# State space mixer: the order of a chunk's work on all engines, forward values in two buffers a chunk ahead, the norm's root on columns

## The chip, the cores and the metric

The kernel runs on one NeuronCore of a Trainium2 chip. The metric is the device time of one launch in microseconds (us), and lower is better. Five engines work side by side: PE (TensorE, the matmuls, with PEld as its weight loads), DVE (VectorE), ACT (ScalarE), POOL (GpSimd) and SP (SyncE, which issues DMAs). Each runs its own instructions strictly in order; semaphores tie them together.

## What is computed

Two transformer-like blocks over 512 tokens and 256 context tokens of width 1024, all in float32. The change touches one of the mixers only, the state space mixer of the first block. Per head h (32 heads of 64 channels, in 4 groups g of 8 heads), per direction d (forward and backward), and per chunk c of 128 tokens:

```python
acs = cumsum(dt * a)                                            # per chunk
chunk_state = einsum('cgs,cge,cgep->geps', bm, exp(a_last - acs), x * dt)
state = exp(a_last) * state + chunk_state                       # chunk by chunk
decay = exp(where(tril, acs_i - acs_j, -inf))
y_diag = einsum('gij,geij,jgep->igep', cm @ bm.T, decay, x * dt)
y_off  = einsum('cgs,geps,cge->cgep', cm, s_start, exp(acs))
...
y = (yf + flip(yb) + d_skip * xs) * silu(z)
yg = y.reshape(tokens, 4, 512)                                  # a group's 512 channels
y = yg * rsqrt(mean(yg * yg, -1) + 1e-6) * norm_w
out = y @ w_out
```

The 256 context tokens give two chunks that only feed the state; the other four chunks give outputs.

## The kernel before

The class `Ssd` makes the mixer. `steps` writes the order down by hand, as one list of steps; every engine walks the whole list and does its own part of each step (`tensor`, `vector`, `scalar`, `pool`, `sync`). So where a step stands in the list sets where it stands on all engines at once. PSUM has eight banks; `banks.take` gives a step a bank, with a wait for whoever read that bank last. The weight panels (`Weights`) are brought by SP, rounded by ACT (`RWH<-RW`, 1.05 us) and their rest is taken by DVE or POOL (`RWr<-RW,RWH`, 1.2 and 2.4 us); where those stand is set by a look-ahead in steps, which the table `calm` shortens in places.

A group g goes through three parts.

- **Convolution.** `cin`, `tap`, `silu`, `ctr`: six column blocks of the input product, taps on DVE, transposes. The steps `third` are the first of the next group's `cin`, cut in three pieces that are put in as filler of PE.
- **States.** For x = 0 to 4, `st` (DVE scales the values into `w1`; PE multiplies, one for each direction) and `sa` (DVE adds to the state). Between them stand the pieces `z` of the gate's product, 12 matmuls of 128x512 each.
- **Chunks**, c = 0 to 3. `ct` and `cb`: small matmuls, whose results ACT copies to `BD`, `NJ` (five small ACTIVATEs) and `cbr`, and POOL masks into `cb`. `gp`: four matmuls with 8 rows into four banks G. `gm`: ACT copies two of the banks to `GG[c % 2]`, DVE takes the minimum with the other two, ACT takes the exponential. `gc`: DVE multiplies that by `cb`, once for each direction, into `GF` (one buffer) and in place (two TENSOR_TENSOR of 128x1024). `xd`: the values times dt, POOL the forward ones, DVE the backward ones. `yd`: 16 matmuls, eight for a direction, with values and masked products. `yo` and `off`: the state's share, on PE, scaled by DVE and added up on POOL in `yy`; `skip` on POOL starts that sum. `ot`: four matmuls that add `yy` to the bank of `yd`. `ya`: DVE multiplies by the gate, ACT squares.

Then the norm, for two halves j of 256 tokens: `ss` on PE sums the squares (four matmuls of 128x256 with the matrix `mean`, which gives every row the sum), ACT takes the root of 128x256 values, DVE their reciprocal (`self.rq`), and `yf` multiplies (DVE), rounds (ACT) and splits (POOL) for the output product `mix`.

The forward values have one buffer (`self.xd[0]`), so POOL's product for chunk c waits until `yd` of chunk c - 1 has read it:

```python
            if c:
                gp.wait_ge("pe.ssd", "yd", g, c - 1)
            else:
                gp.wait_ge("pe.ssd", "S", g, 0, 4)
            gp.wait_ge("v.ssd_dt", "dt")
            gp.tt(self.heads(self.xd[0]), self.heads(self.xs[:, c, :]), self.each(self.DT[:, c, 8 * g:8 * g + 8]),
                  ALU.mult).then_inc("g.ssd_xd", g, c)
            for n in (0, 1) if c == 0 else (c + 1,) if c < 3 else ():
                self.skip(gp, g, n)
```

In the trace nearly everything is recorded in helpers: line 107 is a matmul, 118 and 121 ACTIVATEs, 124 a TENSOR_TENSOR, 138 a reciprocal. The tiles tell the steps apart: `G<-G` and `A<-G,TM` belong to `gm` and `gc`, `PS<-A,TM 128*64` to `yd`. In the group-by-group rows, a matmul in float32 has two records.

Of the kernel before, what the change touches and what calls it, by code (L numbers as in the profile page):

```python
# [1823 lines left out]
class Ssd(Stage):  # L1824
# [6 lines left out]
    def __init__(self, k, gen):  # L1831
# [26 lines left out]
        self.rq = (a(10752, 256), a(11008, 256))  # L1858
# [5 lines left out]
        self.KK = k.dst[:, 0:10]  # L1864
        self.units = [(c, d) for c in range(4) for d in range(2)]

    def steps(self, mixes, mod):
# [4 lines left out]
        last = []  # L1872
        for g in range(4):
# [76 lines left out]
    def tensor(self, p, step, *a):  # L1950
# [94 lines left out]
        elif step == "yd":  # L2045
            g, c = a
            pv = k.banks.take(p, 1, "ssd", "yd", g, c)
            for d, gg in enumerate((self.GF, self.GG[c % 2])):
                p.wait_ge("v.ssd_G", g, c, d)
                p.wait_ge(("g.ssd_xd", "v.ssd_xd")[d], g, c)  # L2050
                for h in range(8):
                    m, half = h // 2, slice(64 * (h % 2), 64 * (h % 2) + 64)
                    last = p.mm(pv[half, 128 * m:128 * m + 128], self.xd[d][:, 64 * h:64 * h + 64], gg[:, h, :],
# [9 lines left out]
        elif step == "ss":  # L2063
# [3 lines left out]
            for m in range(4):  # L2067
                last = p.mm(pv[:, 0:256], k.mean[:, :], self.zz[:, m, 256 * j:256 * j + 256], m == 0, m == 3)
            last.then_inc("pe.ssd", "ss", g, j)

    def scalar(self, s, step, *a):
# [81 lines left out]
        elif step == "gm":  # L2153
# [18 lines left out]
        elif step == "ss":  # L2172
            g, j = a
            if g:
                s.wait_ge("v.ssd_yf", g - 1, j)
# [1803 lines left out]
```

## Time and profile before

| | us |
|---|---|
| median of 3 runs | 4063.89 (4057.85 to 4063.95) |
| the profiled execution | 4055.57 |
| its span | 4053.8 |
| PE busy in it | 3824.3 (94%) |
| DVE, ACT, POOL busy | 1621.4, 1408.8, 1147.2 |

The mixer takes the time from about 1216 to 1875 us of the span. PE carries the chain of waits that ended last (79% of it), so what counts is time in which PE waits or runs at the lower of its two clock levels (2.4 and 1.2 GHz; a granted clock of 1.00 and 0.50). Busy times of PE overlap a little from one matmul to the next, so lengths below are taken from one start to the next.

### The profile page before, as it was taken

The page shows a single profiled execution, that of the slowest core. Times are in us where ns is not written, and L with a number is a line of the kernel's source. Part 1 is how long each engine was busy: PE and PEld are TensorE (multiplying, and loading weights), DVE is VectorE, ACT ScalarE, POOL GpSimd, SP SyncE. Part 2 cuts the span into 40 slices and gives each one's busy share as a digit, 9 for nine tenths or more (in the row PEclk, how much of TensorE's full clock was granted, in tenths as well). Part 3 has the DMA queues.
Part 4 walks back from the last instruction along what each step waited for, and adds up shares of the span by engine and source line. Part 5 has one row for each costly group of instructions (what it writes and reads, how often), then busy time and mean ns, then how long its engine had stood idle before and what let it go on. Part 6 is the DMA issues. An engine that isn't in the chain of part 4 may idle for free.

```text
span 4053.8 us, 52334 instructions
## 1 busy us (share of the span) xinstructions
PE 3824.3 (94%) x22125; PEld 3161.7 (78%) x22125; DVE 1621.4 (40%) x2600; ACT 1408.8 (35%) x2209; POOL 1147.2 (28%) x689
## 2 busy tenths in 40 slices
PE   7999889999999899897999999999998889999999
PEld 5777667888887677676888788888877766688887
DVE  4355573111136666666212321111457843332123
ACT  4223344211125433434422332211455536443223
POOL 2010013111123423425222421211434413243324
PEclk9999999999999999999999999999999999999999
DMA  5221123332333121123333412222322210152333
GB/s 181 73 80 32 58 92 122 97 96 92 96 104 87 33 67 47 33 63 130 107 105 101 151 53 67 64 63 60 117 72 67 59 44 29 55 151 73 99 95 108
DMA packets 472117, 336.66 MB, mean 83 GB/s; under 512 B 17754, under 2 KB 445772, under 8 KB 471884
## 3 DMA queue, kind: packets, MB, share of 16 engines
q1 hardware_dynamic: 471200, 333.06, 27.0%
q8 instruction: 175, 2.87, 0.3%
q14 instruction: 59, 0.48, 0.0%
q10 hardware_dynamic: 683, 0.26, 0.0%
HBM read 331.17 MB, written 2.10 MB: 82 GB/s over the span
## 4 chain that ended last, share of the span: by engine, by line
PE 79%; DVE 8%; ACT 5%; POOL 3%; DMA 2%; issue 2%; SPq 0%; ACTq 0%; POOLq 0%; DVEq 0%
PE PS L107 77%; DVE A L124 2%; PE PS L115 1%; POOL TM L124 1%; ACT A L118 1%; ACT L118 1%; DVE A L132 1%; POOL RWr L124 1%; DMA MW<-in_w_ada 1%; ACT RWH L121 1%; DMA MW<-in_mod_w 1%; DVE TM L132 1%; DVE XT L124 1%; DVE SM L144 1%; ACT TM L118 0%
## 5 line engine op out<-in xcount | busy, mean ns | idle before, releaser
L124 POOL TENSOR_TENSOR RWr<-RW,RWH 128x1024 fp32r<-128x1024 f32 (+2 forms) x316 | 728.4, 2307 | 2235.8 <-ACT RWH L121 2233.1
L107 PE MATMUL PS<-HTH,RWH 128*128 128x512 f32 (+1 forms) x3488 | 1262.7, 362 | 20.8 <-POOL RWr L124 7.6
L107 PE MATMUL PS<-HTH,RWr 128*128 128x512 f32 (+1 forms) x3488 | 1228.1, 352 | 0.0
L107 PE MATMUL PS<-HTr,RWH 128*128 128x512 f32 (+1 forms) x3488 | 1227.9, 352 | 0.0
L107 PE MATMUL PS<-Ar,RWH 128*128 128x512 f32 (+1 forms) x3264 | 819.6, 342 | 20.2 <-DVE XT L132 7.1
L107 PEld LDWEIGHTS PS<-HTH,RWH 128*128 128x128 f32 x3488 | 665.9, 191 | 144.2 <-issue 43.9
L107 PEld LDWEIGHTS PS<-HTr,RWH 128*128 128x128 f32 x3488 | 666.4, 191 | 89.5 <-issue 6.5
L107 PEld LDWEIGHTS PS<-HTH,RWr 128*128 128x128 f32 x3488 | 664.9, 191 | 90.6 <-issue 0.4
L107 PEld LDWEIGHTS PS<-Ar,RWH 128*128 128x128 f32 x3264 | 563.8, 191 | 108.4 <-issue 18.1
L121 ACT ACTIVATE RWH<-RW 128x1024 fp32r<-128x1024 f32 (+2 forms) x474 | 474.8, 1006 | 310.7 <-DMA RW<-in_ffn_w_out 164.9
L107 PE MATMUL PS<-Ar,RWr 128*128 128x512 f32 (+1 forms) x1632 | 552.8, 339 | 0.0
L124 DVE TENSOR_TENSOR A<-A,PS 128x512 f32<-128x512 f32 (+2 forms) x192 | 138.2, 725 | 812.9 <-PE PS L107 801.5
L124 DVE TENSOR_TENSOR RWr<-RW,RWH 128x1024 fp32r<-128x1024 f32 (+2 forms) x158 | 201.5, 1275 | 594.0 <-ACT RWH L121 593.9
L107 PE MATMUL PS<-A 128*128 128x128 f32 (+5 forms) x1820 | 316.8, 360 | 52.8 <-DVE A L124 19.4
L107 PEld LDWEIGHTS PS<-Ar,RWr 128*128 128x128 f32 x1632 | 311.3, 191 | 33.6
L107 PEld LDWEIGHTS PS<-A 128*128 128x128 f32 (+2 forms) x1820 | 216.3, 193 | 137.2 <-issue 66.7
L121 ACT ACTIVATE Ar<-A 128x512 fp32r<-128x512 f32 (+3 forms) x124 | 89.6, 723 | 562.4 <-DVE A L124 529.8
L118 ACT ACTIVATE A<-PS 128x512 f32<-128x512 f32 (+1 forms) x132 | 90.4, 688 | 504.5 <-PE PS L107 492.7
L132 DVE SCALAR_TENSOR_TENSOR XT<-PS,M,XT 128x512 f32<-128x512 f32 (+1 forms) x200 | 117.8, 618 | 275.6 <-PE PS L107 275.3
L121 ACT ACTIVATE A<-PS 128x256 f32<-128x256 f32 (+4 forms) x224 | 115.7, 542 | 278.4 <-PE PS L107 206.2
L118 ACT ACTIVATE A<-A 128x512 f32<-128x512 f32 (+3 forms) x152 | 101.3, 681 | 262.2 <-DVE A L124 175.1
L118 ACT ACT_TABLE_LOAD x129 | 165.5, 1283 | 31.8 <-PE PS L107 18.9
(189 smaller groups left out, 3403.5 us busy)
## 6 DMA issues: line engine op xcount, KB each, us to landing
RW<-in_ffn_w_in SPq DMA_DIRECT2D x176, 512.0 KB, 3.8
MW<-in_mod_w SPq DMA_DIRECT2D x83, 512.0 KB, 4.6
MW<-in_w_ada SPq DMA_DIRECT2D x72, 512.0 KB, 4.5
RW<-in_ffn_w_out SPq DMA_DIRECT2D x64, 512.0 KB, 3.6
RW<-in_ffn_w_out SPq DMA_DIRECT2D x64, 384.0 KB, 3.2
RW<-in_mix_w_in SPq DMA_DIRECT2D x41, 512.0 KB, 3.7
RW<-in_ssd_w_in SPq DMA_DIRECT2D x40, 512.0 KB, 3.9
RW<-in_ev_w_in SPq DMA_DIRECT2D x24, 512.0 KB, 3.8
```

Source lines behind the costliest of these rows:

```text
L107: return self._ins(self.real and self.real.matmul(o, l, r, start=start, stop=stop, skip_group_check=True))
L115: return self._ins(self.real and self.real.transpose(o, i, self.k.ident[0:n, 0:n]))
L118: return self._ins(self.real and self.real.activation(o, i, f, **kw))
L121: return self._ins(self.real and self.real.activation(o, i, ACT.Copy))
L124: return self._ins(self.real and self.real.tensor_tensor(out=o, in0=i0, in1=i1, op=op))
L132: return self._ins(self.real and self.real.scalar_tensor_tensor(out=o, in0=i0, scalar=sc, in1=i1, op0=op0, op1=op1))
L144: return self._ins(self.real and self.real.reduce_max(o, i, AX.X))
```

## The change

Four things change in `Ssd`, and one number in `plan`.

1. `steps`: `gp` of chunk 0 moves out of x = 4 to behind x = 3, with `ct` and `cb` of chunk 1; all eight pieces of `z` now stand in the state steps. `gp` of chunk c + 2 stands at the end of turn c (before, `gp` of chunk c + 1 stood at the start of it). `yo` of chunk c + 1 stands ahead of `yd` of chunk c. The last turn does `ot` and `ya` ahead of the second filler.
2. The step `gx` is new: it holds the two copies by ACT that stood in `gm`, and directly follows `gp`.
3. The forward values get two buffers, `xdf`, and the new function `value` makes chunk c + 1's in the step `xd` of chunk c.
4. The norm's sums become columns: `ss` has eight matmuls that leave 128x1 each, root and reciprocal are taken on 128x2 values, and a new step `sp` spreads them again with two matmuls of 128x128; `yf` reads that bank.
5. `calm`'s entry for the state steps is 12 in place of 24, and covers `gp` of chunk 0.

```diff
-        self.rq = (a(10752, 256), a(11008, 256))
+        self.root = (k.dst[:, 12:14], k.dst[:, 14:16])
+        self.xdf = (work[:, 0:512], a(10752, 512))
...
             for x in range(5):
-                out += one("st", g, 0, x) + one("st", g, 1, x)
-                out += one("gp", g, 0) + one("yo", g, 0) if x == 4 else z[x + 3]
-                out += one("sa", g, 0, x) + one("sa", g, 1, x)
-            out += one("gm", g, 0) + z[7] + one("yo", g, 1) + one("xd", g, 0) + one("off", g, 0) + one("off", g, 1)
-            out += one("ct", g, 1) + one("cb", g, 1) + one("yo", g, 2) + one("yo", g, 3)
+                out += one("st", g, 0, x) + one("st", g, 1, x) + z[x + 3] + one("sa", g, 0, x) + one("sa", g, 1, x)
+                if x == 3:
+                    out += one("gp", g, 0) + one("gx", g, 0) + one("ct", g, 1) + one("cb", g, 1)
+            out += one("gm", g, 0) + one("yo", g, 0) + one("yo", g, 1) + one("gp", g, 1) + one("gx", g, 1) + one("xd", g, 0)
...
-                turn = one("gp", g, c + 1) if more else self.filler(g, 0, mod)
-                turn += one("gc", g, c) + one("yd", g, c)
+                turn = [] if more else self.filler(g, 0, mod)
+                if c == 0:
+                    turn += one("off", g, 0) + one("off", g, 1)
+                turn += one("gc", g, c)
                 if more:
-                    turn += one("off", g, 2 * c + 2) + one("gm", g, c + 1) + one("off", g, 2 * c + 3)
-                else:
-                    turn += self.filler(g, 1, mod)
+                    turn += one("yo", g, 2 * c + 2) + one("yo", g, 2 * c + 3) + one("gm", g, c + 1)
+                turn += one("yd", g, c)
+                if more:
+                    turn += one("off", g, 2 * c + 2) + one("off", g, 2 * c + 3)
                 if c < 2:
                     turn += one("ct", g, c + 2) + one("cb", g, c + 2)
-                turn += one("ot", g, c) + one("ya", g, c)
                 if more:
                     turn += one("xd", g, c + 1)
+                turn += one("ot", g, c) + one("ya", g, c)
                 if c < 2:
-                    turn += one("yo", g, 2 * c + 4) + one("yo", g, 2 * c + 5)
+                    turn += one("gp", g, c + 2) + one("gx", g, c + 2)
                 if c == 2:
                     turn += one("ss", g, 0)
                 if c == 3:
-                    turn += one("yf", g, 0)
+                    turn += self.filler(g, 1, mod) + one("sp", g, 0) + one("yf", g, 0)
                 turns.append(turn)
-            turns += [one("ss", g, 1), one("yf", g, 1)]
+            turns += [one("ss", g, 1), one("sp", g, 1) + one("yf", g, 1)]
...
-            for m in range(4):
-                last = p.mm(pv[:, 0:256], k.mean[:, :], self.zz[:, m, 256 * j:256 * j + 256], m == 0, m == 3)
+            for c in range(2):
+                for m in range(4):
+                    at = 256 * j + 128 * c
+                    last = p.mm(pv[:, c:c + 1], self.zz[:, m, at:at + 128], k.ones[:, 0:1], m == 0, m == 3)
...
+            p.wait_ge("v.ssd_rs", g, j)
+            for c in range(2):
+                last = p.mm(pv[:, 128 * c:128 * c + 128], self.root[j][:, c:c + 1].to_broadcast([128, 128]), k.ident,
+                            True, True)
...
+    def value(self, gp, g, c):
...
+        if c > 1:
+            gp.wait_ge("pe.ssd", "yd", g, c - 2)
+        else:
+            gp.wait_ge("pe.ssd", "S", g, 1, 4)
+        gp.tt(self.heads(self.xdf[c % 2]), self.heads(self.xs[:, c, :]), self.each(self.DT[:, c, 8 * g:8 * g + 8]),
+              ALU.mult).then_inc("g.ssd_xd", g, c)
...
-            k.w.calm.update((i, 24) for i, step in enumerate(steps) if step[0] is ssd and (
-                step[1] == "z" and step[3] or step[1] in ("st", "sa") and step[4]))
+            k.w.calm.update((i, 12) for i, step in enumerate(steps) if step[0] is ssd and (
+                step[1] == "z" and step[3] or step[1] in ("st", "sa") and step[4] or step[1] == "gp" and not step[3]))
```

DVE in the last two turns of group 0, before, from `gc` of chunk 2 on: `A<-A,PS` or `G<-G,PS` is `gm`, `TM<-PS,TM` and `A<-PS,TM` are `off` of the two directions, `A<-PS,A` is `ya`, `TM<-A,TM` is `xd`, `A<-A,TM 128x1024` is `gc`.

```order
747 L124 TENSOR_TENSOR A<-G,TM 128x1024
748 L124 TENSOR_TENSOR G<-G,TM 128x1024
749 L124 TENSOR_TENSOR TM<-PS,TM 128x512
750 L124 TENSOR_TENSOR A<-A,PS 128x512 x2
751 L124 TENSOR_TENSOR A<-PS,TM 128x512
752 L124 TENSOR_TENSOR A<-PS,A 128x4x128
753 L124 TENSOR_TENSOR TM<-A,TM 128x512
754 L138 RECIPROCAL A<-A 128x256
755 L124 TENSOR_TENSOR RWr<-RW,RWH 128x1024
756 L124 TENSOR_TENSOR A<-A,TM 128x1024 x2
757 L124 TENSOR_TENSOR A<-PS,A 128x4x128
758 L132 SCALAR_TENSOR_TENSOR A<-A,VEC 128x256 x4
```

The same place on DVE after:

```order
747 L124 TENSOR_TENSOR A<-G,TM 128x1024
748 L124 TENSOR_TENSOR G<-G,TM 128x1024
749 L124 TENSOR_TENSOR A<-A,PS 128x512 x2
750 L124 TENSOR_TENSOR TM<-PS,TM 128x512
751 L124 TENSOR_TENSOR A<-PS,TM 128x512
752 L124 TENSOR_TENSOR TM<-A,TM 128x512
753 L124 TENSOR_TENSOR A<-PS,A 128x4x128
754 L124 TENSOR_TENSOR RWr<-RW,RWH 128x1024
755 L124 TENSOR_TENSOR A<-A,TM 128x1024 x2
756 L124 TENSOR_TENSOR A<-PS,A 128x4x128
757 L138 RECIPROCAL SM<-SM 128x2
758 L132 SCALAR_TENSOR_TENSOR A<-A,VEC,PS 128x256 x4
```

The minimum now stands ahead of both `off`, `xd` ahead of `ya`, and the reciprocal, now 128x2, behind the last `gc` and `ya`.

POOL in the chunks of group 1, before: `TM<-A,CC` masks `cb`, the first of `TM<-A,TM` is the forward value, the next the skip; `TM<-TM`, `TM<-TM,A`, and `A<-A,TM`, `A<-A` are `off`'s sums (an `A<-A,TM` ahead of them is a skip too).

```order
78 L124 TENSOR_TENSOR TM<-A,TM 128x512 x2
79 L124 TENSOR_TENSOR A<-A,TM 128x512
80 L124 TENSOR_TENSOR TM<-TM 128x512
81 L124 TENSOR_TENSOR TM<-TM,A 128x512
82 L124 TENSOR_TENSOR TM<-A,CC 128x256
83 L124 TENSOR_TENSOR A<-A,TM 128x512
84 L124 TENSOR_TENSOR A<-A 128x512
85 L124 TENSOR_TENSOR TM<-A,CC 128x256
86 L124 TENSOR_TENSOR TM<-A,TM 128x512 x2
87 L124 TENSOR_TENSOR TM<-TM 128x512
```

POOL, the same place after:

```order
77 L124 TENSOR_TENSOR TM<-A,TM 128x512 x2
78 L124 TENSOR_TENSOR A<-A,TM 128x512
79 L124 TENSOR_TENSOR TM<-TM 128x512
80 L124 TENSOR_TENSOR TM<-TM,A 128x512
81 L124 TENSOR_TENSOR A<-A,TM 128x512 x2
82 L124 TENSOR_TENSOR A<-A 128x512
83 L124 TENSOR_TENSOR TM<-A,CC 128x256
84 L124 TENSOR_TENSOR TM<-A,TM 128x512 x2
85 L124 TENSOR_TENSOR TM<-TM 128x512
```

The first three rows are now the value and skip of chunk 0 and the value of chunk 1; the skip of chunk 1 has moved behind the first two sums, and only one mask stands between the sums of chunk 1 and the next value, which is chunk 2's (row 84; row 86 of before is chunk 1's).

## Rows read from the trace of the kernel before

**Rows 1.** Windows of the four chunk stretches: from:to, length, busy by engine, granted clock, DMA.

```profile
1354.20:1404.10 49.90, 41.27 (x283) 28.70 (x283) 33.61 (x34) 24.86 (x45) 31.07 (x21) 0.86 0.07 22
1511.20:1557.50 46.30, 38.57 (x282) 26.58 (x282) 33.74 (x35) 24.74 (x45) 31.47 (x21) 0.93 0.07 24
1663.20:1710.90 47.70, 38.84 (x282) 26.53 (x282) 34.58 (x35) 24.81 (x45) 31.45 (x21) 0.93 0.07 23
1816.40:1850.70 34.30, 28.96 (x220) 18.15 (x220) 27.81 (x30) 22.28 (x43) 31.01 (x21) 0.95 0.09 32
```

**Rows 2.** Timeline, PE, group 1: start, us, form, count, idle before and releaser.

```profile
1511.18 2.20 PE L107 MATMUL PS<-A 8*128 8x512 f32 x10
1512.81 0.79 PE L107 MATMUL PS<-HTH,RWH 128*128 128x512 f32 x1
...
1515.99 1.02 PE L107 MATMUL PS<-A 128*128 128x512 f32 x2
...
1520.82 1.09 PE L107 MATMUL PS<-A,TM 128*64 128x128 f32 x16
...
1522.71 0.41 PE L107 MATMUL PS<-CC,TM 128*8 128x128 f32 x8
...
1530.24 3.40 PE L107 MATMUL PS<-A,TM 128*64 128x128 f32 x32 [2.71 <-POOL TM L124]
...
1539.32 1.33 PE L107 MATMUL PS<-A,TM 128*64 128x128 f32 x16 [1.25 <-ACT A L121]
...
1543.83 1.89 PE L107 MATMUL PS<-A,mean 128*128 128x256 f32 x8
...
1551.72 1.53 PE L107 MATMUL PS<-A,TM 128*64 128x128 f32 x20 [3.27 <-DVE A L124]
```

**Rows 3.** Timeline, POOL, group 1: value of chunk 1 and skip of chunk 2.

```profile
1528.07 3.02 POOL L124 TENSOR_TENSOR TM<-A,TM 128x512 f32<-128x512 f32 x2
```

**Rows 4.** Timeline, DVE, group 1: `gm`, `xd`, `gc` of chunk 1, reciprocal, `gc` of chunk 3.

```profile
1521.89 1.27 DVE L124 TENSOR_TENSOR A<-A,PS 128x512 f32<-128x512 f32 x2
...
1525.08 1.32 DVE L124 TENSOR_TENSOR TM<-A,TM 128x512 f32<-128x512 f32 x1
1526.32 2.88 DVE L124 TENSOR_TENSOR A<-A,TM 128x1024 f32<-128x1024 f32 x2
...
1547.21 1.75 DVE L138 RECIPROCAL A<-A 128x256 f32<-128x256 f32 x1 [1.66 <-ACT A L118]
1548.88 3.87 DVE L124 TENSOR_TENSOR A<-A,TM 128x1024 f32<-128x1024 f32 x2
```

**Rows 5.** Timeline, PE, group 0: `yd` of chunk 1.

```profile
1374.48 3.68 PE L107 MATMUL PS<-A,TM 128*64 128x128 f32 x32 [3.27 <-POOL TM L124]
```

**Rows 6.** Timeline, ACT, group 1: table load and exponentials, then `ct`'s five.

```profile
1513.49 1.28 ACT L118 ACT_TABLE_LOAD   x1
1514.79 1.16 ACT L118 ACTIVATE G<-G 128x512 f32<-128x512 f32 x2
...
1524.40 1.84 ACT L118 ACTIVATE A<-PS,SM 128x128 f32<-128x128 f32 x5
```

**Rows 7.** Timeline, two layer norms: sums, modulation row, root, reciprocal, spread.

```profile
1223.64 1.84 PE L107 MATMUL PS<-ones,TM 128*128 128x1 f32 x16
1225.41 0.64 PE L107 MATMUL PS<-MW,CS 128*32 128x256 f32 x8
...
1904.99 0.26 ACT L118 ACTIVATE SM<-PS,cols 128x2 f32<-128x2 f32 x1 [1.37 <-PE PS L107]
1905.28 0.17 DVE L138 RECIPROCAL SM<-SM 128x2 f32<-128x2 f32 x1 [0.66 <-ACT SM L118]
...
1907.58 0.71 PE L107 MATMUL PS<-CC,SM 128*128 128x128 f32 x4
```

**Rows 8.** Timeline, PE, group 3 behind its chunks: a modulation row.

```profile
1864.72 0.64 PE L107 MATMUL PS<-MW,CS 128*32 128x256 f32 x8 [1.85 <-DMA MW<-in_w_ada]
```

**Rows 9.** Windows of PE around two waits of 1.25 us: busy, clock.

```profile
1540.00:1543.40 3.40, 3.40 (x29) 0.51 0.02 5
...
1844.00:1847.20 3.20, 1.95 (x30) 1.00 0.00 0
```

More of the change, by code:

```diff
@@ L2050, in tensor @@
                 p.wait_ge(("g.ssd_xd", "v.ssd_xd")[d], g, c)
+                xd = self.xd[1] if d else self.xdf[c % 2]
                 for h in range(8):
                     m, half = h // 2, slice(64 * (h % 2), 64 * (h % 2) + 64)
-                    last = p.mm(pv[half, 128 * m:128 * m + 128], self.xd[d][:, 64 * h:64 * h + 64], gg[:, h, :],
+                    last = p.mm(pv[half, 128 * m:128 * m + 128], xd[:, 64 * h:64 * h + 64], gg[:, h, :],
                                 not d and h < 2, False)
@@ L2066, in tensor @@
             p.wait_ge("s.ssd_sq", g, 2 * j + 1)
-            for m in range(4):
-                last = p.mm(pv[:, 0:256], k.mean[:, :], self.zz[:, m, 256 * j:256 * j + 256], m == 0, m == 3)
+            for c in range(2):
+                for m in range(4):
+                    at = 256 * j + 128 * c
+                    last = p.mm(pv[:, c:c + 1], self.zz[:, m, at:at + 128], k.ones[:, 0:1], m == 0, m == 3)
             last.then_inc("pe.ssd", "ss", g, j)
+        elif step == "sp":
+            g, j = a
+            pv = k.banks.take(p, 1, "ssd", "sp", g, j)
+            p.wait_ge("v.ssd_rs", g, j)
+            for c in range(2):
+                last = p.mm(pv[:, 128 * c:128 * c + 128], self.root[j][:, c:c + 1].to_broadcast([128, 128]), k.ident,
+                            True, True)
+            last.then_inc("pe.ssd", "sp", g, j)
     def scalar(self, s, step, *a):
@@ L2163, in scalar @@
                     "s.ssd_gb", g, c, x).frees("ssd", "G", g, c, 2 + x)
+        elif step == "gm":
+            g, c = a
+            gg = self.GG[c % 2]
             for x in range(2):
@@ L2173, in scalar @@
             g, j = a
-            if g:
-                s.wait_ge("v.ssd_yf", g - 1, j)
             s.wait_ge("pe.ssd", "ss", g, j)
-            s.act(self.rq[j], k.banks.of("ssd", "ss", g, j)[:, 0:256], ACT.Sqrt, bias=k.epsc, scale=2.0).then_inc(
+            s.act(self.root[j], k.banks.of("ssd", "ss", g, j)[:, 0:2], ACT.Sqrt, bias=k.epsc, scale=1.0 / 512).then_inc(
                 "s.ssd_rs", g, j).frees("ssd", "ss", g, j)
@@ L2267, in vector @@
             if i % 2 == 0:
-                if g and i == 0:
-                    v.wait_ge("v.ssd_yf", g - 1, 1)
                 v.wait_ge("pe.ssd", "ctr", g, i)
@@ L2347, in vector @@
                  self.zz[:, :, cs], ALU.mult).then_inc("v.ssd_y", g, c).frees("ssd", "yd", g, c)
-        elif step == "ss":
+        elif step == "sp":
             g, j = a
             v.wait_ge("s.ssd_rs", g, j)
-            v.rcp(self.rq[j], self.rq[j]).then_inc("v.ssd_rs", g, j)
+            v.rcp(self.root[j], self.root[j]).then_inc("v.ssd_rs", g, j)
         elif step == "yf":
@@ L2377, in pool @@
             g, c = a
-            self.xs_ready(gp, g)
-            if c:
-                gp.wait_ge("pe.ssd", "yd", g, c - 1)
-            else:
-                gp.wait_ge("pe.ssd", "S", g, 0, 4)
-            gp.wait_ge("v.ssd_dt", "dt")
-            gp.tt(self.heads(self.xd[0]), self.heads(self.xs[:, c, :]), self.each(self.DT[:, c, 8 * g:8 * g + 8]),
-                  ALU.mult).then_inc("g.ssd_xd", g, c)
             for n in (0, 1) if c == 0 else (c + 1,) if c < 3 else ():
-                self.skip(gp, g, n)
+                self.value(gp, g, n)
+                if n != 1:
+                    self.skip(gp, g, n)
         elif step == "off":
@@ L2394, in pool @@
             gp.tt(yy, yy, self.yo[d], ALU.add).then_inc("g.ssd_off", g, i)
+            if i == 1:
+                self.skip(gp, g, 1)
         elif step == "yf":
```

10 lines of the change are left out of this document (6 added, 4 removed).

## Prediction

> **What bounds the kernel now.** Start with the table: PE is busy 94% of the span, and the chain of waits runs through it. So the question is how long PE waits in the stretches that the change touches, and at which clock it runs there. I read four views in this order. The windows [rows 1] cut out the chunk stretch of each group, from the start of `gp` of chunk 0 to the start of the third `third` piece (in group 3 to the first modulation matmuls): 49.9, 46.3, 47.7 and 34.3 us, at granted clocks of 0.86, 0.93, 0.93 and 0.95. PE is busy 8.6, 7.7, 8.9 and 5.3 us less than that. The timeline of PE [rows 2, 5] names the waits of a group: 2.71 us (3.27 in group 0) ahead of `yd` of chunk 1, released by POOL (the forward value), 1.25 ahead of `yd` of chunk 2, released by ACT (the exponential), 3.27 ahead of `yd` of chunk 3, released by DVE (`gc`). The other engines' timelines say why. POOL starts value 1 at 1528.07 [rows 3], since it had to wait for `yd` of chunk 0, and needs half of 3.02. DVE starts the last `gc` only after a reciprocal of 1.75 which itself waited 1.66 for the root [rows 4]. The clock: a mean clock of 0.86 means 28% of the time at half speed, and work done at half speed loses half of its time, 14% of the whole. So 49.9 x 0.14 = 7.0, 46.3 x 0.07 = 3.2, 47.7 x 0.07 = 3.3 and 34.3 x 0.05 = 1.7 us are lost at most, 15.3 in all, in some 30.6 us at the lower level (1.2 GHz).
>
> **Change 1 to 3: the chunks.** Count from t = 0, the end of the last state matmul. `gp` 0, `ct` 1 and `cb` 1 now stand ahead of it; they are 1.14 (a `gp` is 8 records), 0.35 and 0.35, so a stretch has 1.85 to its credit that is only moved. PE then does z7, which takes 3.2 (1512.81 to 1515.99, [rows 2]), `yo` 0 and 1 (1.02 by two records, 0.95 each by starts): 5.1, `gp` 1: 6.2, `yo` 2 and 3: 8.1. On ACT the gate's SiLU follows z7 (0.6, half of a pair's 1.16), then a table load of 1.28 and the exponential of chunk 0, 1.16 [rows 6]: 6.45. Before, that exponential ran beside z7. Now it is the first link, and what is late behind it is `gc`. A `gc` pair took 2.88 and 3.87 beside POOL [rows 4]; I take 3.7 for chunk 0, where POOL has two values, a mask and skips to do: 10.15. `yd` 0 starts with its forward half and waits for the second: it ends at 11.1, after a wait of about 1.1.
>
> Then each turn repeats. DVE: `gm` 1.2 (1.27 as a pair [rows 4]), two `off` 1.2, `xd` 1.0 (0.65 to 1.32), `ya` 0.6, `gc` 3.8: 7.8. PE in the same turn: `ct` 0.35, wait for ACT's five small ACTIVATEs (1.84 [rows 6], with 0.35 of latency on both sides), `gp` 1.1, two `yo` 1.9, `yd` 1.9, `cb` and `ot` inside the ACT time: about 7.4. The first is longer, so DVE carries the turn. Before, the two `yo` stood between `ct` and `gp` and hid the five ACTIVATEs; now about 1.3 us of PE's waiting stands ahead of `gp` of chunk c + 2. The forward value drops out: POOL makes it a chunk ahead, at a time when it waits for nothing on DVE or PE but `yd` of two chunks earlier. It is queued behind fewer steps than before, and two skips wait behind it, for which only `off`'s sums, half a turn later, wait. Two turns end at 25.75. Behind the third `gc` come `gm`, `off`, `xd` and `ya` of the next chunk (4.0) and ACT's square (0.65, half of 1.23 or less): `ss` 0 starts at 30.5, after a wait of some 2.3, since `ya` 2 now stands behind `xd` 3. From there on PE has `ss` 1.77, filler 2.77 (12 matmuls by 0.23), `yd` 3 1.85, `ot` 0.95, filler 2.77, with no wait: the reciprocal is no longer ahead of `gc`, which needs 3.87 from 30 on and has 4.5. End: 40.6, with the credit 42.45. Group 3 ends its stretch behind `ss`: 1.85 + 30.5 + 1.77 = 34.1.
>
> At full clock throughout, that is 49.9 - 42.45 = 7.45, then 3.85, 5.25 and 0.2: **16.7 us** less.
>
> A rule of the Trainium skill speaks on these links. A `gc` pair took 2.88 in one place and 3.87 in another, beside POOL in both [rows 4]. The Trainium skill (SBUF — State Buffer, SBUF: two separate sides) says that DVE and GpSimd take a shared port pair as an exclusive lock, for a whole instruction; two rows of different length agree with that, and by it a `gc` that starts beside two POOL products could take up to two of POOL's, each 1.0 to 1.5, more; rival D would then be the likeliest.
> The other rule is on the table: the exponential starts 0.02 us behind the end of the 1.28 of the load [rows 6]. The Trainium skill (ScalarE: Activation LUTs, What ACT_TABLE_LOAD costs) has a drain of some 1.38 us beside the load, 2.66 in all. The trace disagrees, and leaves this no chance; by the page, `ss` 0 would stand 1.4 later in each group, and 5.5 of the gain would be gone.
>
> **Change 4: the norm.** `ss` has 16 records of one column in place of 8 of 256. Sixteen such took 1.77 (1223.64 to 1225.41 [rows 7]) where the old form took 1.54 (1.89 less the overlap of 0.35 at the next start): +0.23 for each half, already in the stretch for half 0. The spreads: four records took 0.71, 0.54 by starts [rows 7]: 2 x 0.54. `sp` 0 stands behind filler and waits for nothing. `sp` 1 follows `ss` 1 at once, and PE waits for its own end, the root 0.26, two handovers and the reciprocal 0.17 [rows 7]: about 0.65 (between 0.3, if only the two operations count, and 2.3, the 1.37 and 0.66 of idle time in these rows added to them, a path with more in it). Before, the next group's `cin` followed `ss` 1 and hid the long root and reciprocal. Sum for a group: 1.08 + 0.23 + 0.65 = 1.96, three times **5.9**. In group 3 PE waits for DMA ahead of modulation rows (1.85, [rows 8]) and the addition lies under that: 0. Two table loads per group go; none was waited for.
>
> **Change 5: `calm`.** A look-ahead of 12 moves some roundings and rests; no DMA is added. No PE wait for a weight stood in the stretches. One `RWH` (1.05, in the words on the weight panels) ahead of an exponential would cost as much, once per group; one that goes away gains as much. I take 0, and +4 to -4 for the range.
>
> **The clock.** The waits of a group shrink from about 7.6 to 6.3 by my walk (1.1, 1.3, 1.3, 2.3), and the long ones of 2.7 to 3.3 are gone. What the clock does with that isn't shown by one row: after a wait of 1.25 that came soon behind a longer one it stands at 0.51 for 3.4 us, around an equal one in group 3 at 1.00 [rows 9]. I take one such stretch of 3.4 for a group, behind the 2.3: 1.7 x 4 = **6.8** lost.
>
> **Sum.** 16.7 - 5.9 - 6.8 = 4 us less. The profiled execution took 4055.6 with a span of 4053.8, and is 8.3 below the median of the runs shown and 2.3 below the lowest; the difference is carried over to the median as it is: 4063.9 - 4 = **4060**.
>
> **Rivals.** *Faster (B).* Both uncertain terms fall well: shorter waits leave the clock up (2 lost instead of 6.8), and the turns go at PE's 7.4 as `gc` comes nearer to 2.88 (POOL's work is spread evener): 2 x 0.4 x 4 = 3.2. Gain 16.7 + 3.2 - 5.9 - 2 = 12; with the first `gc` also at 2.9, 3 more. 4049 to 4052. For it: full clock around the single 1.25. Against: four waits a group still.
> *Slower (C).* One mechanism, the clock in the chunks: the chip answers to each of the new waits with 3.4 us at the lower level, since they stand 6 to 8 us apart, as the waits in group 1 did [rows 9]. Each costs 1.7. The sum without clock is 10.8; slower by over 8 us needs 19, that is 11 of them; three for a group, 12, cost 20.4: 4073.5. All 16 give 4080. Against: before, waits of 7.6 in a group led to at most 7 us of loss.
> *It doesn't do what it says (D).* The value's wait goes, but the turn stays as long because `gc` on DVE, with POOL's value and skip beside it, ends no sooner: turns of 9, as now (from 1530.24 to 1539.32 [rows 2]). Two turns of 9 instead of 7.8 cost 2.4 x 4 = 9.6: gain 4 - 9.6, 4069.5.
>
> **How the numbers follow.** A measurement of this kernel tells from no change what is over 0.2%, 8.1 us. My sum (A) has 0.45, with its own range of 4055 to 4069; B 0.36; C 0.11; D 0.08. A reaches into faster a little, D into slower half: faster 0.39, same 0.45, slower 0.16. The range from 4046 to 4073 leaves out the outer third of B and most of C.
>
> **What would show it.** In the profile after: no wait on POOL ahead of `yd` 1; a wait of about 1.1 on DVE inside `yd` 0, of 1.3 on ACT ahead of each `gp` of chunks 2 and 3, of 2.3 on ACT ahead of `ss` 0, none ahead of `yd` 3; `sp` 1 with 0.65 on DVE; stretches of about 42.5 us, and 34 in group 3; 8 table loads fewer. Wrong are the steps whose wait differs by over 0.5. The forecast as a whole fails if the clock of the stretches after rises to 0.98 or more (B) or falls below 0.9 (C), or if the turns aren't near 7.8.

## The result and the profile after

The changed kernel takes 4040.0 us (median of 4 runs, 4038.3 to 4042.2) beside 4063.9 before: the ratio is 0.9949 with a 95% interval of 0.9935 to 0.9963, some 21 us (15 to 26). That is faster, by more than what such a measurement can tell from no change, and it lies below the predicted range, which ended at 4046. The forecast of 4060 said no change.

The profiled execution took 4042.2, with a span of 4040.4; before it was 4055.6. So the two profiles lie 13.4 us apart, and the medians 24. The first question is which steps of the walk failed in the 13.4, the second what became of the rest.

The chunk stretches of the changed kernel, from about the start of z7 (the last piece of the gate's product) to the start of the third filler piece (in group 3 to the end of `ss` 0; the cuts are up to 0.3 us off these starts), with the columns of [rows 1]:

```profile
1358.30:1401.30 43.00, 36.78 (x278) 25.45 (x277) 31.94 (x36) 19.44 (x39) 27.23 (x19) 0.96 0.08 25
1515.00:1553.30 38.30, 35.40 (x280) 24.18 (x279) 31.59 (x35) 19.70 (x39) 29.57 (x20) 1.00 0.09 29
1662.50:1700.80 38.30, 35.40 (x280) 24.19 (x279) 31.57 (x35) 19.69 (x39) 29.55 (x20) 1.00 0.08 28
1810.30:1840.30 30.00, 27.09 (x224) 17.02 (x226) 28.27 (x33) 16.15 (x35) 26.87 (x19) 1.00 0.11 37
```

The clock stands at 1.00 in three of the four, where it was 0.93, 0.93 and 0.95. PE is idle 6.2, 2.9, 2.9 and 2.9 us in them, where it was 8.6, 7.7, 8.9 and 5.3.

PE's timeline in group 1 (start, length, form, count, idle before and releaser), which answers to [rows 2]; the first row is in the state part, the next two are `yd` 0's two halves. The row of 28 records at 1528.75 is `gp` 2, two `yo` and the first half of `yd` 1, and 1532.66 is the second half of `yd` 1. Then come `gp` 3 with two `yo`, the first half of `yd` 2, `ss` 0, the first half of `yd` 3, `sp` 0, `ss` 1 and `sp` 1:

```profile
1505.29 3.13 PE L107 MATMUL PS<-TM,A 128*128 128x512 f32 x4 [1.92 <-DVE TM L124]
...
1522.96 1.09 PE L107 MATMUL PS<-A,TM 128*64 128x128 f32 x16
1525.06 1.09 PE L107 MATMUL PS<-G,TM 128*64 128x128 f32 x16 [1.01 <-DVE G L124]
...
1528.75 4.08 PE L107 MATMUL PS<-A 8*128 8x512 f32 x28 [0.95 <-DVE TM L124]
1532.66 1.07 PE L107 MATMUL PS<-A,TM 128*64 128x128 f32 x16
...
1536.33 3.05 PE L107 MATMUL PS<-A 8*128 8x512 f32 x12 [0.95 <-ACT A L118]
...
1539.32 1.09 PE L107 MATMUL PS<-A,TM 128*64 128x128 f32 x16
...
1542.39 1.84 PE L107 MATMUL PS<-ones,A 128*128 128x1 f32 x16
...
1547.03 1.09 PE L107 MATMUL PS<-A 128*64 128x128 f32 x16
...
1552.70 0.61 PE L107 MATMUL PS<-CC,SM 128*128 128x128 f32 x4
...
1556.02 1.84 PE L107 MATMUL PS<-ones,A 128*128 128x1 f32 x16
...
1558.42 0.71 PE L107 MATMUL PS<-CC,SM 128*128 128x128 f32 x4 [0.55 <-DVE SM L138]
```

The wait for POOL ahead of `yd` 1 is gone, and so is that of 3.27 ahead of `yd` 3. There are three waits of about 1 us in the chunks, one of 0.55 for the reciprocal, and a new one of 1.92 in the state part. For the wait ahead of `gp` 2 the row names DVE, but the DVE product that ends there is `xd` 1 (1527.32 to 1528.70), for which `gp` doesn't wait. In both places it needs ACT's five small ACTIVATEs, which end 0.14 us ahead of it:

```profile
1526.77 1.84 ACT L118 ACTIVATE A<-PS,SM 128x128 f32<-128x128 f32 x5
...
1534.35 1.84 ACT L118 ACTIVATE A<-PS,SM 128x128 f32<-128x128 f32 x5
```

Nothing stands ahead of `ss` 0, where the prediction had put 2.3.

The stretches are not all of the mixer. Outside them the clock still falls, behind `sp` 1 of group 0 (after a wait of 0.55 only), behind the 1.92 in the states of group 1, and at the end of group 3. The last three figures of a row are the granted clock, the DMA share and GB/s:

```profile
1405.50:1413.00 7.50, 6.95 (x28) 0.77 0.20 65
1505.20:1512.00 6.80, 6.63 (x20) 0.75 0.00 0
1853.70:1862.00 8.30, 6.81 (x38) 0.59 0.26 86
```

By the way the prediction counts (length times what the clock falls short of 1), these are 1.7, 1.7 and 3.4 us.

Group 0 alone still waits long ahead of `yd` 3. PE first, then DVE at the same place: the weight's rest stands ahead of `gc`, and has itself waited 3.22 for its rounding on ACT:

```profile
1393.46 1.47 PE L107 MATMUL PS<-A 128*64 128x128 f32 x16 [3.35 <-DVE A L124]
1394.65 1.99 PE L107 MATMUL PS<-A,TM 128*64 128x128 f32 x16
```

```profile
1387.10 0.68 DVE L124 TENSOR_TENSOR A<-PS,A 128x512 f32<-128x512 f32 x1
1391.00 1.23 DVE L124 TENSOR_TENSOR RWr<-RW,RWH 128x1024 fp32r<-128x1024 f32 x1 [3.22 <-ACT RWH L121]
```

To compare whole mixers I take the time from the last transposes ahead of the states of group 0 (1331.57 before, 1331.91 after) to the first sums of the next norm (1888.72 and 1874.82). It holds all four groups, and no row of it depends on where a stretch is cut.

| kernel | median, us | ratio to before (95%) | mixer in its profile | clock of the stretches |
|---|---|---|---|---|
| before | 4062 to 4064 | 1 | 557.2 | 0.86 0.93 0.93 0.95 |
| before, another execution | (4073.2, one run) | | 563.3 | 0.93 0.89 0.87 0.91 |
| changed | 4040.0 | 0.9949 (0.9935 to 0.9963) | 542.9 | 0.96 1.00 1.00 1.00 |
| changed, another execution | (4042.3, one run) | | 544.5 | 1.00 1.00 1.00 1.00 |

### The profile page after: what moved, and what is told of

It is laid out like the page before. It is cut to its first block, busy times and chain, and to the rows that moved or that the text cites. A ratio compares the mean times of both kernels' runs of the same rounds, so it can differ in the third digit from the quotient of the medians.

```text
span 4040.4 us, 52541 instructions
## 1 busy us (share of the span) xinstructions
PE 3823.2 (95%) x22221; PEld 3162.3 (78%) x22221; DVE 1614.3 (40%) x2600; ACT 1396.4 (35%) x2201; POOL 1151.6 (29%) x689
## 4 chain that ended last, share of the span: by engine, by line
PE 79%; DVE 8%; ACT 5%; DMA 3%; issue 2%; POOL 2%; SPq 0%; ACTq 0%; DVEq 0%; POOLq 0%
PE PS L107 77%; DVE A L124 2%; PE PS L115 2%; ACT A L118 1%; DVE A L132 1%; ACT L118 1%; POOL RWr L124 1%; DMA MW<-in_w_ada 1%; DVE TM L124 1%; DMA MW<-in_mod_w 1%; ACT RWH L121 1%; POOL TM L124 1%; DVE TM L132 1%; DVE SM L144 1%; DMA RW<-in_ssd_w_in 0%
## 5 line engine op out<-in xcount | busy, mean ns | idle before, releaser
L107 PE MATMUL PS<-A 128*128 128x128 f32 (+7 forms) x1948 | 322.6, 352 | 57.4 <-DVE A L124 22.6
L107 PEld LDWEIGHTS PS<-A 64*128 64x128 f32 (+3 forms) x1948 | 223.1, 188 | 145.2 <-issue 68.5
```

The source lines that it names most:

```text
L107: return self._ins(self.real and self.real.matmul(o, l, r, start=start, stop=stop, skip_group_check=True))
```

## Experiments

**1. Spare matmuls in the waits of the kernel before.** How much of the time is clock? PE is given useless work in two waits of each group (in group 3 in one), and nothing else is touched.

```diff
             pv = k.banks.take(p, 1, "ssd", "yd", g, c)
+            for _ in range((0, 6, 0, 7 if g < 3 else 0)[c]):
+                p.mm(pv[:, 0:256], k.ident, k.CC[:, 0:2, :].rearrange("p a b -> p (a b)"), True, True)
             for d, gg in enumerate((self.GF, self.GG[c % 2])):
```

> The kernel before, with spare matmuls of 128x256 put on PE into the two long waits of each group: six ahead of yd of chunk 1, seven ahead of yd of chunk 3 (in groups 0 to 2), written to the bank of yd, which the first real matmul starts anew. Nothing else is changed, so PE has about 2.3 and 2.7 us more to do in waits of 2.2 to 3.3. Theory one (what the change gained is mostly clock: PE falls to 1.2 GHz after the long waits): the chunk stretches show a clock of 0.97 or more in place of 0.86 to 0.95, and the kernel is 8 to 14 us faster though it does more. Rival (the gain is in the waits themselves, and the clock follows from something else): the clock of the stretches stays, or the time stays within 3 us, since every wait still ends when POOL or DVE is done.

Measured: 4046.7 us, ratio 0.9957 (0.9940 to 0.9974), 17 us faster. The mixer takes 550.6. The windows of its stretches (the last figures of a row are the granted clock, the DMA share and GB/s):

```profile
1355.30:1401.00 45.70, 43.16 (x309) 0.96 0.07 24
1506.70:1551.70 45.00, 43.01 (x310) 0.96 0.08 25
1657.30:1702.50 45.20, 41.52 (x309) 1.00 0.08 24
1808.10:1840.80 32.70, 30.15 (x232) 1.00 0.11 34
```

The operands come no sooner (the waits left are of 0.2 to 0.5, the 1.25 ahead of `yd` 2 and one of 1.94 ahead of `gp` 1 in group 2, which stood there before as 1.95), and still the stretches are 4.2, 1.3, 2.5 and 1.6 us shorter, with more matmuls in them. So a long wait costs more than its own length: the seven that were filled were 20.6 us together, and 17 us come back in the median though their length stays. Theory one holds, and with a larger size than the profile of before suggested. The clock of the stretches is 0.96 in two, just short of the 0.97 expected. The median's gain of 17 is above the 8 to 14 expected, though the interval (11 to 24) reaches into them; the mixer of the profile gives 6.5 to 12.5 of it, depending on which execution of before it is compared with.

**2. The norm alone, and 3. the norm with two value buffers,** both in the old order of the chunks.

```diff
-            turns += [one("ss", g, 1), one("yf", g, 1)]
+            turns += [one("ss", g, 1), one("sp", g, 1) + one("yf", g, 1)]
...
+        self.xdf = (work[:, 0:512], a(10752, 512))
...
-            if c:
-                gp.wait_ge("pe.ssd", "yd", g, c - 1)
+                self.value(gp, g, n)
```

(The first pair of lines stands for all of change 4 and is in both kernels, the rest for all of change 3 and only in the second.)

> The kernel before with the norm's part of the change alone (sums in columns, root and reciprocal on 128x2, spread by sp; the order of the chunks as before). Theory one: the reciprocal of 1.75 and its wait for the root leave DVE's way ahead of the last gc, the wait of yd of chunk 3 falls from 3.2 to about 1 in groups 0 to 2, and the clock behind it stays up: 6 for the waits and up to 5 for the clock gained, 5 paid for sp and ss: 3 to 7 us faster. Rival: the spread costs what the wait gives, 0 plus or minus 2.

> The same with the forward values in two buffers and a chunk ahead as well (the order of the chunks as before). Theory one: POOL's wait for yd of chunk 0 goes, but gc of chunk 1 is done only about 1 us ahead of the value before, so the wait ahead of yd of chunk 1 falls by about 1 us in each group, from 3.3 and 2.7 to about 2, and the clock behind it may stay up in some: 4 to 10 us faster than the norm's part alone. Rival (the second buffer is what the change lives on): the wait goes altogether and the two parts alone give the 20 us of the whole change.

Measured: the norm alone 4053.9, ratio 0.9972 (0.9961 to 0.9984), 11 us; with the two buffers 4046.9, ratio 0.9952 (0.9935 to 0.9970), 19 us. PE in group 1 of the first, then of the second kernel, ahead of `yd` 1:

```profile
1526.98 1.97 PE L107 MATMUL PS<-A,TM 128*64 128x128 f32 x32 [2.71 <-POOL TM L124]
```

```profile
1520.03 1.09 PE L107 MATMUL PS<-A 128*64 128x128 f32 x16 [0.82 <-DVE A L124]
1521.61 1.97 PE L107 MATMUL PS<-A,TM 128*64 128x128 f32 x16 [0.48 <-DVE A L124]
```

With a second buffer POOL is no longer the releaser, and one wait of 2.71 becomes two, 0.82 and 0.48, for `gc`. The wait falls by 1.4 here, and by 1.1 on the mean of the four groups, where about 1 was expected. Ahead of `yd` 3 no row of a wait is left in group 1 of either, where it was 3.27 (in group 0 it is 1.8, where it was 2.72). So each part takes away one of the two long waits, and both together have 19 of the 21 us without any change in the order. The second buffer is worth 7 to 8 us beyond the norm, inside theory one's 4 to 10, though the two intervals overlap; but the rival's other half, that the two parts come to the whole gain, is not excluded by these runs. The expectation of 3 to 7 for the norm alone was low. Its own profiled mixer, 562.1, doesn't show the gain at all; it drew a low clock in group 2. That one execution can't decide between kernels 10 us apart is what run 5 is about.

**4. The changed kernel with one buffer.**

```diff
-            for n in (0, 1) if c == 0 else (c + 1,) if c < 3 else ():
-                self.value(gp, g, n)
-                if n != 1:
-                    self.skip(gp, g, n)
+            self.value(gp, g, c)
+            if c != 3:
+                self.skip(gp, g, c + 1 if c else 0)
...
-        if c > 1:
-            gp.wait_ge("pe.ssd", "yd", g, c - 2)
+        if c:
+            gp.wait_ge("pe.ssd", "yd", g, c - 1)
```

> The changed kernel with one buffer for the forward values again (POOL makes chunk c's in the step xd of chunk c, once yd of chunk c - 1 is done). Theory one (the order needs the second buffer): value 1 starts only after yd 0, behind which the mask and sums stand, so yd 1 waits 1 to 2.5 us on POOL in each group, with the clock behind it: 8 to 16 us slower than the changed kernel. Rival (in the new order gp and yo stand between two yd and leave POOL the time): within 3 us of the changed kernel.

Measured: 4043.2, ratio 0.9954 (0.9937 to 0.9970), 3 us behind the changed kernel and not to be told from it by the intervals. PE in group 1:

```profile
1530.56 1.97 PE L107 MATMUL PS<-A,TM 128*64 128x128 f32 x32 [1.81 <-POOL TM L124]
1534.93 3.06 PE L107 MATMUL PS<-A 8*128 8x512 f32 x12 [0.75 <-DVE A L124]
1538.75 1.09 PE L107 MATMUL PS<-A,TM 128*64 128x128 f32 x16 [0.77 <-POOL TM L124]
```

Half of each theory. The wait for POOL is there, 1.81, as theory one said; but the clock of the stretches is 1.00, so the wait costs itself and nothing behind it. The window of group 1, from behind z7:

```profile
1511.00:1553.00 42.00, 35.98 (x284) 1.00 0.08 26
```

The waits in the chunks of group 1 are 6.0 us together, where the changed kernel has 2.9, and in the profile the mixer is 12 us longer (555.0). The median, only 3 us longer, goes with the rival. The table behind run 10 shows how the two fit: the six runs are 9 us longer on the mean when lost clock is left out, and lost 3 us less of clock than the changed kernel.

**5. Both kernels once more, as they are.**

> The kernel before once more, unchanged, for another profiled execution. The two profiles so far lie 13 us apart, the medians 24. Theory one (the clock is drawn anew in each execution, and the first profile of before was a lucky one): other stretches of the same kernel show another clock, and the mixer takes 557 us plus 2 to 8. Rival (the mixer takes the same in every execution, the difference lies in other stages): 557 within 1.

> The changed kernel once more, unchanged. Theory one: the mixer within 2 us of 542.9, since its stretches have a clock of 1.00 and nothing is left to draw but in group 0, after the wait of 3.35. Rival: it varies as much as that of the kernel before.

Measured: before 4073.2 with a mixer of 563.3, changed 4042.3 with 544.5, both as theory one had it. Windows of before, cut as [rows 1]:

```profile
1357.20:1404.50 47.30, 39.17 (x282) 0.93 0.07 24
1510.40:1558.30 47.90, 39.76 (x283) 0.89 0.07 23
1664.10:1715.30 51.20, 41.97 (x283) 0.87 0.07 22
1821.00:1857.40 36.40, 30.52 (x219) 0.91 0.09 30
```

The same instructions, and another clock in each: what a stretch loses by clock is 3.3, 5.3, 6.7 and 3.3, in all 18.6, where the first execution had 15.3. In the 52 runs of before made beside these experiments the time went from 4042.5 to 4075.4, in the five of the changed kernel from 4038.3 to 4042.3. Of the 17.5 us between the two spans of before, 6.1 are in the mixer and 3.1 lie ahead of it; the other 8.4 are in stages behind it that the change doesn't touch. The profile on which the prediction stood was an execution near the fast end (only 7 of the 52 runs were faster).

In the second execution of the changed kernel the wait of group 0 stands as before, and the clock doesn't fall behind it:

```profile
1398.35 1.09 PE L107 MATMUL PS<-A 128*64 128x128 f32 x16 [3.33 <-DVE A L124]
```

```profile
1397.00:1404.60 7.60, 6.25 (x57) 1.00 0.01 2
```

So a wait of 3.3 us doesn't bring the lower clock each time.

**6. The order alone:** steps, `gx` and the look-ahead, with one buffer and the old norm.

```diff
...
-                    last = p.mm(pv[:, c:c + 1], self.zz[:, m, at:at + 128], k.ones[:, 0:1], m == 0, m == 3)
+                last = p.mm(pv[:, 0:256], k.mean[:, :], self.zz[:, m, 256 * j:256 * j + 256], m == 0, m == 3)
...
```

(against the kernel of run 4; root, reciprocal and `yf` as before the change.)

> The kernel before with the new order alone (steps, gx apart from gm, the look-ahead number 12), but one buffer for the forward values and the norm's old form on 128x256. Theory one (the order is worth most, as in the changed kernel with one buffer, and the old norm costs 2 to 4 more, since its reciprocal stands ahead of the last gc again but the last turn now has ot and ya ahead of the second filler): ratio 0.996 to 0.998, 8 to 16 us faster than before. Rival (each part is worth a third, none alone shows much): under 5 us.

Measured: 4058.0, ratio 0.9982 (0.9968 to 0.9995), 7 us faster, just below the 8 to 16. PE in group 1, ahead of `yd` 3:

```profile
1548.73 3.31 PE L107 MATMUL PS<-A,TM 128*64 128x128 f32 x32 [3.27 <-DVE A L124]
```

The 3.27 stands as it stood before, to the hundredth: the order does nothing for it, since the reciprocal is still ahead of the last `gc`. The order and the norm together (run 4) give 19, where alone they gave 7 and 11.

**7 and 8. The look-ahead number, and the rest in group 0.** First the number back to 24, then with it the rest of group 0 behind `gc`.

```diff
-            k.w.calm.update((i, 12) for i, step in enumerate(steps) if step[0] is ssd and (
+            k.w.calm.update((i, 24) for i, step in enumerate(steps) if step[0] is ssd and (
...
+            k.w.calm.update((i, 60) for i, step in enumerate(steps) if step[0] is ssd and tuple(step[1:]) in (
+                ("ss", 0, 0), ("third", 1, 0), ("gc", 0, 3)))
```

> The changed kernel with the look-ahead number of the state steps at 24 again, as before the change. On ACT two roundings of weights then stand behind one SiLU of the gate in place of ahead of it, in each group; on DVE one rest of group 1 and 3 moves by one x. Theory one (12 brings two rests on POOL beside DVE's scalings, which stretches them from 0.7 to 2.8, and PE waits 1.92, 1.92, 0.57 and 1.50 us): those waits go, 4 to 6 us faster in the state parts, unless POOL's rests come to lie ahead of value 0, which would cost 1 to 2 in yd 0. Rival: the rests come later and cost the chunks as much, within 2 us of the changed kernel.

> The same with 24, and the weight's rest of DVE in group 0 behind the last gc in place of ahead of it (it stood there with 3.2 us of waiting for its rounding). Theory one (this rest alone is why yd of chunk 3 waits 3.35 in group 0 and not in the others): that wait goes, and the clock of 0.96 in that stretch rises to 1.00: 4 to 5 us faster than with 24 alone. Rival: gc there is late for another reason, under 1 us.

Measured: 4047.4, ratio 0.9970 (0.9956 to 0.9983), and 4042.7, ratio 0.9956 (0.9942 to 0.9971). The first is 7 us slower than the changed kernel, against both theories; the second takes 5 back, as its theory one had it. The intervals of neighbours touch or overlap, so these two steps rest on the profiles: the mixer takes 555.7 in the first and 546.2 in the second. PE, DVE and ACT of the first in the states of group 1:

```profile
1510.47 3.78 PE L107 MATMUL PS<-TM,A 128*128 128x512 f32 x4 [3.91 <-DVE TM L124]
```

```profile
1506.35 1.22 DVE L124 TENSOR_TENSOR RWr<-RW,RWH 128x1024 fp32r<-128x1024 f32 x1 [3.66 <-ACT RWH L121]
1507.49 2.83 DVE L124 TENSOR_TENSOR TM<-A,TM 128x512 f32<-128x512 f32 x1
```

```profile
1504.78 0.60 ACT L118 ACTIVATE A<-PS 128x512 f32<-128x512 f32 x1 [12.86 <-PE PS L107]
1505.27 1.99 ACT L121 ACTIVATE RWH<-RW 128x1024 fp32r<-128x1024 f32 x2
```

With 24 ACT's two roundings stand behind a SiLU for which it waits 12.86; DVE's rest waits 3.66 for them, and the scalings of the state behind the rest. So in groups 1 and 2 PE's wait rises to 3.91 and 4.01. In groups 0 and 3, where both rests are POOL's, it sinks from 1.92 and 1.50 to 0.38. The number is right for two groups and wrong for two, either way. In the second kernel, with the rest behind `gc`, the way from `ss` 0 to the third piece in group 0 takes 10.67 us as in groups 1 and 2, in place of 15.71.

**9. Both put together by group:** 24 in groups 0 and 3, 12 in groups 1 and 2, the rest of group 0 behind `gc` (the lines for that are those of run 8).

```diff
-            k.w.calm.update((i, 12) for i, step in enumerate(steps) if step[0] is ssd and (
+            k.w.calm.update((i, 24 if step[2] in (0, 3) else 12) for i, step in enumerate(steps) if step[0] is ssd and (
```

> The changed kernel with the rest of group 0 behind the last gc, and the look-ahead number by group: 24 in groups 0 and 3, where it took PE's wait in the states from 1.9 and 1.5 to 0.4, and 12 in groups 1 and 2, where 24 made it 3.9 and 4.0. Theory one (the wait in the states hangs on whether DVE's rest stands ahead of a scaling and its rounding behind the gate's SiLU, group by group): the mixer takes 542.9 - 5.0 (group 0's last turn) - 1.5 - 1.1 = 535 in the profile, 6 to 8 us less than the changed kernel in the median too. Rival (what is gained there is lost at the next wait): within 3 us of the changed kernel.

Measured: **4028.8**, ratio 0.9907 (0.9892 to 0.9922), 35 us faster than before and 11 faster than the changed kernel, above the 6 to 8 expected; its mixer takes 535.5, where 535 was expected. This version beats both. DVE in group 0 now, `ya` 2, `gc` 3, then the rest:

```profile
1388.44 0.68 DVE L124 TENSOR_TENSOR A<-PS,A 128x512 f32<-128x512 f32 x1
1389.04 2.85 DVE L124 TENSOR_TENSOR A<-A,TM 128x1024 f32<-128x1024 f32 x2
1392.35 1.23 DVE L124 TENSOR_TENSOR RWr<-RW,RWH 128x1024 fp32r<-128x1024 f32 x1 [0.46 <-ACT RWH L121]
```

**10. The second spread behind the next column block,** on top of that.

```diff
-                out += last[0] + one("pads", g) + one("third", g, 2) + last[1] + last[2] + cin[1]
+                out += last[0] + one("pads", g) + one("third", g, 2) + last[1] + cin[1] + last[2]
```

> The same with the second spread of the norm behind the next group's second column block in place of ahead of it. Theory one: PE's wait of 0.55 us for the reciprocal goes in groups 0 to 2, and the product waits for nothing else: 1.5 to 2 us faster than with it ahead. Rival (the normed values are late then, and the output product or the next SiLU waits for them): the same or slower.

Measured: 4046.0, ratio 0.9950 (0.9936 to 0.9964): 17 slower than run 9. The 0.55 is gone, and PE waits ahead of `mix` for the split values, 5.69, 5.69 and 5.68 in groups 0 to 2, which are 17 us together. The row of group 0:

```profile
1406.07 1.19 PE L107 MATMUL PS<-Ar,RWH 128*128 128x512 f32 x2 [5.69 <-POOL Ar L124]
```

The rival holds: what is queued behind `sp` 1 on DVE, ACT and POOL (`yf`, the rounding, the split) was on PE's way after all.

**All runs: clock and the rest.** Each run is on record with its span and its mean granted clock, so the span can be split in two: span times what the clock falls short of 1 is lost by clock, the remainder is what waits and work would take at full clock. That is an estimate: the clock has three places on record, 2 us for a single run, and a low clock during a wait costs nothing. Means of the runs:

| kernel | runs | time | lost by clock | rest |
|---|---|---|---|---|
| before | 52 | 4062.8 | 101 | 3960 |
| changed | 5 | 4040.6 | 81 | 3958 |
| 1, spare matmuls | 6 | 4046.9 | 82 | 3963 |
| 2, norm alone | 12 | 4052.7 | 93 | 3958 |
| 3, norm, two buffers | 6 | 4045.4 | 89 | 3955 |
| 4, changed, one buffer | 6 | 4045.8 | 78 | 3967 |
| 6, order alone | 12 | 4056.2 | 86 | 3969 |
| 9, number by group | 5 | 4027.6 | 73 | 3953 |

So of the 22 us that the change gives, 20 are clock and 2 are less waiting and work. Run 1 gives back the same 19 of clock without bringing any operand sooner. The order alone makes the rest 9 us longer and wins 15 of clock; with the norm and the second buffer the rest comes back down.

## Why the prediction was wrong

The steps that failed are the wait of 2.3 us ahead of `ss` 0, which isn't there; the state parts, taken as unchanged, which became 6.4 longer; and the clock, where the kernel got back 20 us by the runs and the prediction had 8.5 (15.3 lost before, 6.8 after). By its own terms, in the profiled executions first (4 us forecast, 13.4 measured, 14.2 of it in the mixer):

| term, us gained | forecast | measured |
|---|---|---|
| chunk stretches, at full clock after | 16.7 | 25.9 |
| clock lost in the stretches after | -6.8 | -1.7 |
| norm, groups 0 to 2 | -5.9 | -6.2 |
| states, with the look-ahead | 0 | -6.4 |
| group 3 behind `ss` 0 | 0 | 2.6 |
| sum | 4 | 14.2 |

The 16.7 are called "at full clock", but the lengths of before in them hold the 15.3 that before lost by clock. So the walk itself forecast only 1.4 us less of waits and work in the stretches.

- **Chunks up to `yd` 2: right.** z7 to the end of `yd` 0 was put at 11.1, and is 11.1 (1515.00 to 1526.08). The wait in `yd` 0 was put at 1.1 and is 1.01. Two turns of 7.8 were forecast; from one end of `yd` to the next they take 7.58 and 7.73, so D is excluded. The waits ahead of `gp` are 0.95, not 1.3, behind ACT's five ACTIVATEs as forecast. The table load is followed by the exponential without a gap, as before (load at 1518.98 for 1.28, exponential at 1520.27), and there are 8 loads fewer (121 for 129).
- **`ss` 0: the step that failed in the walk.** "`ss` 0 starts at 30.5, after a wait of some 2.3, since `ya` 2 now stands behind `xd` 3." The sums of half 0 need the squares of chunks 0 and 1 only, which are the first 256 tokens, and both are long done. It starts at 27.4 (1542.39). With the 1.73 that was moved put back and `sp` 0's 0.36 left to the norm, the stretches of groups 1 to 3 are 6.9, 8.4 and 3.4 us shorter than before, where 3.85, 5.25 and 0.2 were forecast: 3.1 to 3.2 too little in each, which is this step.
- **The clock: the mis-sized term.** I counted 6.8 lost in the stretches. Measured is 43.0 x 0.04 = 1.7 in group 0, behind the 3.35 that I had not foreseen, and 0 in the others. Waits of 1 us, three in a row, their ends 3.7 and 7.6 us apart, left the clock at 1.00. Rival B had this right, C was excluded. (The waits named in the prediction add up to 6.0, not to its 6.3.) Outside the stretches another 6.8 were lost, in the three places shown above, where before had 1.7, in the states of group 1; no term of mine covered these. In these two executions the mixer therefore gained 8.6 by clock, near the forecast 8.5, though not where it was forecast: that match is luck. The runs as a whole gained 20.
- **`yd` 3 in group 0.** That there would be no wait from there on held in three groups. In group 0 a weight's rest takes the place of the reciprocal ahead of `gc`: 3.35 us and the 1.7 of clock. The order shown ahead of the prediction is that of group 0 and has it, at row 754; I priced the reciprocal that left and not the rest that stayed, and took the wait as gone in all groups.
- **The states: unpriced.** I took 0 for the look-ahead, between -4 and +4. The state parts became 1.8, 2.5, 0.8 and 1.3 us longer beyond what was moved into them, 6.4 in all, mostly the waits of 1.92, 1.92, 0.57 and 1.50; in group 1 the clock behind the wait comes on top. Runs 7 to 9 show the cause: with the other look-ahead number the waits of groups 0 and 3 go down to 0.38. That of group 1 is there with either number.
- **The norm: right in sum, in part by luck.** 5.9 were forecast. From the start of the third piece to the next group's transposes it is 2.6, 1.3 and 1.3 longer, and `sp` 0 adds 0.36 three times: 6.2. But 1.7 of the 2.6 in group 0 are clock, so the norm itself is some 4.5. `sp` 1 waits 0.55 for 0.65. In group 3, taken at nothing, the end behind `ss` 0 is 2.7 shorter counted from its start (37.1 for 39.8): the waits there (for modulation rows, the norm and the split) come to 4.6 in place of 8.8, and 3.4 are lost by clock that before didn't lose.
- **Profile to median: the other half of the miss.** "The difference is carried over to the median as it is." The first profile of before was 8.3 us below its median, the changed kernel's is 2.2 above. The table of all runs says what that difference is: before loses 101 us by clock on the mean, and its first profile had lost some 92 (a clock of 0.977), a lucky draw, while the changed kernel's profile had lost 81, its mean. So the 8.3 belonged to the gain, or at least into the range on the fast side. Where in the kernel the clock of the medians was won isn't shown: 8.4 us of the difference between two executions of before were in stages that the change leaves alone.

So the time went the way B said, at a size that no case had, since none had the missing `ss` 0 wait and the offset together. What the parts gave, by the ratios, each to within some 6 us: the norm 11, the order 7, norm and second buffer 19, norm and order 19, all three 21. Norm and order add up; the second buffer adds 8 in the old order and 2 in the new. Why those two overlap wasn't tested.

## What to carry to other kernels

Ask of each wait on PE how long it is, since a long one was often paid twice here, once as idle time and again in clock; the change turned 2.7 and 3.3 into pieces of about 1, and the clock in the chunks stayed up. Where a wait can't be shortened, spare matmuls in it gave most of the same gain. Split the time of each run into lost clock and the rest before crediting a part with it: the order alone made the rest longer and was faster all the same.

Before a step's wait is priced, write down which values it reads (here chunks 0 and 1, not 2), and read the order in every group: what a planner puts ahead of a critical instruction differs from group to group.

One profiled execution of a kernel that loses clock is one draw. How far it is from the median belongs in the range.

## What the runs showed of the hardware

- One TENSOR_TENSOR of 128x512 on DVE takes 0.6 to 0.7 us. Beside a weight's rest on POOL of 3.31 us (1501.37 in group 1 of the changed kernel) the same took 2.85:


```profile
1501.24 1.22 DVE L124 TENSOR_TENSOR RWr<-RW,RWH 128x1024 fp32r<-128x1024 f32 x1
1502.38 2.85 DVE L124 TENSOR_TENSOR TM<-A,TM 128x512 f32<-128x512 f32 x1
```

It is 2.2 longer, about what was left of POOL's instruction when it began, and its next, of the same form, took 0.68. That agrees with what the Trainium skill (SBUF — State Buffer, SBUF: two separate sides) says of a shared port pair that is held for a whole instruction. The last `gc` pair, with POOL's rest beside it in [rows 4], went the other way, from 3.87 to 2.85 (the row of run 9).
- The clock was granted in full through three waits of about 1 us in each of three groups. In the kernel of run 4 it was granted in full through more and longer ones, in group 1 six of together 6.0, the longest 1.81. Behind a wait of 3.35 it fell in one execution of the changed kernel, and behind the same wait (3.33) it stayed at 1.00 in the other. It fell behind a 0.55 in group 0. So length alone doesn't settle it, and no run here shows what does. In the kernel of run 3, whose longest wait in group 1 was 1.11 but which has two pairs of waits close together (0.82 and 0.48, 1.11 and 0.84), the clock was 0.92:

```profile
1502.90:1547.00 44.10, 39.41 (x295) 0.92 0.07 25
```

- The time of the kernel before varied by 33 us over 52 runs, with a mean granted clock of 0.970 to 0.980, and mostly with that clock: the rest of the table above had a standard deviation of 3.7 us in them, the time 6.5. The changed kernel stayed within 4 us in five runs, but the kernel of run 1, without the long waits, still varied by 14 in six. So that only long waits make the time vary isn't shown.
